# Three projections that carry the small stages behind them, and eight taps of a convolution on TensorE

## What is computed

```python
def nsa(h, w_in, ...):            # D = 1024, kv = 256, 16 heads
    q, kc, vc, ks, vs, kw, vw, gates = jnp.split(h @ w_in, splits, axis=-1)
    kc, vc = compress(kc, ...), compress(vc, ...)
    gates = jax.nn.sigmoid(gates)                       # 3 per head
    return (g0 * o_cmp + g1 * o_sel + g2 * o_win) @ w_out

def conformer_conv(val, gate, conv_w, ...):             # 31 taps, 512 channels
    u = val * jax.nn.sigmoid(gate)
    y = causal_depthwise_conv(u, conv_w) + conv_b
    return jax.nn.silu(layer_norm_2(y, ln_g, ln_b))

def fox_mix(h, w_in, fgate_b, q_g, k_g, w_out):
    q, k, v, fz = jnp.split(h @ w_in, [hd, 2 * hd, 3 * hd], axis=-1)
    q, k = rms_norm(heads(q), q_g), rms_norm(heads(k), k_g)
    c = jnp.cumsum(jax.nn.log_sigmoid(fz + fgate_b), axis=1)
    # causal softmax of q.k * scale + c[query] - c[key], times v, @ w_out

def third_mix(y, ...):
    q, k, v, gu, gv = jnp.split(y @ w_in, ...)          # 512 each
    attn_out = moba_attention(rope(q), rope(k), v)
    gv = layernorm(gelu(gv), gmlp_ln_g, gmlp_ln_b)
    gmlp_out = gelu(gu) * (causal(w_s) @ gv + b_s)      # per head, chunks of 128
    return concat([rmsnorm(attn_out, g_a), rmsnorm(gmlp_out, g_g)]) @ w_out
```

## Time and profile before

| | us |
|---|---|
| median of three runs | 4069.65 |
| lowest and highest | 4064.81, 4070.16 |
| the profiled execution | 4067.28 |
| its span | 4065.5 |
| PE busy | 3757.7 (92%) |
| DVE busy | 2986.4 (73%) |
| ACT busy | 1814.9 (45%) |
| mean TensorE clock granted | 0.953 |

### The profile page before, as it was taken

One profiled execution on the slowest core, in us unless ns is written; L12 is line 12 of the kernel. 1 busy time (PEld: TensorE's weight loads), 2 busy tenths in 40 slices (PEclk: granted clock), 3 DMA queues, 4 the chain that ended last, 5 costly groups with the idle time before them and its releaser, 6 DMA issues. The chain is left out here.

```text
span 4065.5 us, 72114 instructions
## 1 busy us (share of the span) xinstructions
PE 3757.7 (92%) x29143; PEld 3408.6 (84%) x29143; DVE 2986.4 (73%) x5894; ACT 1814.9 (45%) x3679; POOL 346.3 (9%) x259
## 2 busy tenths in 40 slices
PE   6999899997899769999999997998999999998698
PEld 6987799996799659989998885898999988897597
DVE  7876778785787677987677856589776787787665
ACT  3444445442454444434444454443444444544343
POOL 0000000000000004830000000086100000000000
PEclk9999899998799879999999997999999999999799
DMA  8766476764166414434444443343444444675253
GB/s 322 277 233 251 172 263 240 264 257 167 57 254 254 155 42 177 153 129 168 172 170 167 158 175 114 114 169 134 146 167 172 171 156 177 244 300 211 94 180 142
DMA packets 119358, 748.70 MB, mean 184 GB/s; under 512 B 13681, under 2 KB 13841, under 8 KB 43761
## 3 DMA queue, kind: packets, MB, share of 16 engines
q1 hardware_dynamic: 117506, 739.92, 49.6%
q10 hardware_dynamic: 688, 3.11, 0.2%
q0 software_dynamic: 832, 1.06, 0.1%
HBM read 741.93 MB, written 1.05 MB: 183 GB/s over the span
## 5 line engine op out<-in xcount | busy, mean ns | idle before, releaser
L930 ACT ACTIVATE weights_high<-weight_ring 128x512 fp32r<-128x512 f32 x2248 | 1294.6, 624 | 1225.6 <-PE bank L196 909.2
L938 DVE TENSOR_TENSOR weights_low<-weight_ring,weights_high 128x512 fp32r<-128x512 f32 x2016 | 1297.1, 686 | 613.4 <-ACT weights_high L930 607.8
L196 PE MATMUL bank<-h_high,weights_high 128*128 128x256 f32 x4800 | 1370.7, 286 | 31.7 <-DVE h_low L682 10.3
L196 PE MATMUL bank<-h_low,weights_high 128*128 128x256 f32 x4800 | 1362.7, 284 | 0.0
L196 PE MATMUL bank<-h_high,weights_low 128*128 128x256 f32 x4800 | 1362.3, 284 | 0.0
L196 PEld LDWEIGHTS bank<-h_high,weights_high 128*128 128x128 f32 x4800 | 924.8, 193 | 51.3 <-issue 27.4
L196 PEld LDWEIGHTS bank<-h_low,weights_high 128*128 128x128 f32 x4800 | 925.4, 193 | 8.7 <-issue 0.2
L196 PEld LDWEIGHTS bank<-h_high,weights_low 128*128 128x128 f32 x4800 | 924.9, 193 | 0.0
L196 PE MATMUL acc<-weights_high,hidden_high 128*128 128x512 f32 x1552 | 613.3, 395 | 0.0
L196 PE MATMUL acc<-weights_low,hidden_high 128*128 128x512 f32 x1552 | 606.4, 391 | 0.0
L196 PE MATMUL acc<-weights_high,hidden_low 128*128 128x512 f32 x1552 | 604.2, 389 | 0.0
(11 more groups left out here) (297 smaller groups left out, 3460.3 us busy)
## 6 DMA issues: line engine op xcount, KB each, us to landing
weight_ring<-stream SPq DMA_DIRECT2D x580, 1024.0 KB, 4.8
h_tok<-slots SPq DMA_DIRECT2D x100, 512.0 KB, 5.8
h_feat<-slots SPq DMA_DIRECT2D x90, 512.0 KB, 5.8
work<-slots SPq DMA_DIRECT2D x26, 512.0 KB, 8.4
mod_sums<-biases SPq DMA_DIRECT2D x7, 1536.0 KB
h_feat<-rows SPq DMA_DIRECT2D x8, 512.0 KB, 4.1
work<-biases SPq DMA_DIRECT2D x1, 1536.0 KB
x_tok<-x ACTq DMA_DIRECT2D x1, 1024.0 KB, 5.4
```

Source lines behind the costliest of these rows:

```text
L196: ins = self.nc.tensor.matmul(out, lhs, rhs, start=start, stop=stop)
L930: act.activation(k.w_hi[:, b, q * self.QUARTER:(q + 1) * self.QUARTER], self.raw(g, q), ACT.Copy).then_inc(k.highs_ready, 1)
L938: return eng.tensor_tensor(k.w_lo[:, b, w], self.raw(g, q), k.w_hi[:, b, w].bitcast(F32), ALU.subtract)
```

## The change

- NSA: the narrow stage goes. `ToFeatureRowsAndGates` makes the 16 f32 products of the gates in four parts, behind the products of halves 8 to 11, into another bank, and ScalarE takes the sigmoid from there behind half 11. Their weights are no longer in the slot stream: `DirectRows` loads them in front of slot s + 3. The features stage sums twelve modulation slots from half 6 on, the tokens stage none. The four row copies of GpSimd move to the `Scores` of the first branch, the compressed branch comes last.
- Even mix: the last eight taps of channel block 2 leave VectorE. ScalarE makes eight more diagonals at the end of `GlaDecays`, TensorE does eight f32 products of 128x256 between key and value products of `GlaAttend`, VectorE adds the result at its end.
- Fox: `ToTokens`, `ToTokensNarrow`, `HeadNorm` and `ForgetGates` become `ToNormedHeads`. VectorE multiplies by the gains as it evicts, ScalarE squares, VectorE reduces block by block; root, scaling, gates, cumulative sums and the filling of constant rows are set to single halves.
- Third mix: `ToTokens`, both `Keep`, `Rope`, `Spatial` and the second `HeadRms` become `ToTokensAndGate`, whose columns come in the order gv, gu, q, k, v. The causal mask of the mixing weights comes at half 3, layer norm at halves 4 to 8, spatial products behind half 10, gates at 10 and 12, norm at 13 to 16, rotation of the two token tiles at 17 and 18. It sums four slots; `third_ffn(0)` sums 14 in halves 50 to 66.

The stream has 575 slots instead of 581, and 49 stages end in a barrier instead of 58. The core of the diff:

```diff
+class DirectRows:
+    def issue(self, sp, biases, slots, rows):
+        self.host.wait_begun(sp)
+        for i, place in enumerate(self.places):
+            n = place.shape[1]
+            sp.dma_start(place, rows[self.first + i][:, 0:n]).then_inc(self.k.direct_landed, 16)
...
+class ToFeatureRowsAndGates(ToFeatureRows):
+    FIRST = 8
+    def products(self, pe, g, hi, lo):
+        k, part = self.k, g - self.FIRST
+        super().products(pe, g, hi, lo)
+        if part == 0:
+            self.direct.wait(pe)
+        if 0 <= part < 4:
+            t, half, w = part // 2, part % 2, self.gates.shape[2]
+            for kk in range(half * DC // 2, (half + 1) * DC // 2):
+                mm = k.mm(k.acc[:, t, 0:w], k.h_t[:, kk, t * P:(t + 1) * P], self.kept[:, kk * w:(kk + 1) * w],
+                          start=kk == 0, stop=kk == DC - 1, last=True)
...
+class ToNormedHeads(ToTokens):
+    def vector_after(self, dve, g):
...
+        elif g % 4 == 3:
+            for t in range(TT):
+                a = slice(b * 512, (b + 1) * 512)
+                dve.wait_ge(k.scalar_for_vector.sem, k.scalar_for_vector.take())
+                dve.tensor_tensor(self.qk[:, t, a], k.bank[:, (TT * b + t) % NB, :], self.gains[:, a],
+                                  ALU.mult).then_inc(k.vector_for_tensor.sem, k.vector_for_tensor.send())
+        if g % 4 == 0 and 0 < b <= self.N:
...
+            ins = dve.tensor_reduce(stat, squares, AX, ALU.add)
...
+        self.gates.vector(dve, g)
+        piece = g - 4 * self.N - 2
+        if 0 <= piece < 4:
...
+            dve.tensor_tensor(heads, heads, self.stat[:, at:at + n // 2].unsqueeze(2).to_broadcast([P, n // 2, HD]),
+                              ALU.mult)
...
 class Convolve:
+    LATE = 8
...
+    def late_products(self, pe):
+        k, c = self.k, CONV // P - 2
+        for i in range(self.LATE):
+            tap = TAPS - self.LATE + i
+            pe.wait_ge(k.diagonals, TAPS + i + 1)
+            mm = k.mm(k.acc[:, 3, 0:S], self.late[i], self.u[:, c, tap:tap + S], start=i == 0,
+                      stop=i == self.LATE - 1, last=True)
...
+class ToTokensAndGate(ToTokens):
+    def vector_after(self, dve, g):
+        k = self.k
+        super().vector_after(dve, g)
+        if g == 3:
+            self.keep(dve)
+        if 4 <= g <= 8:
+            self.norm(dve, g - 4)
+        if g == 10:
...
+            self.gate(dve, 0)
+        if g == 12:
+            self.gate(dve, 1)
+        if 13 <= g <= 16:
+            self.root_mean_square(dve, g - 13)
+        if g == 17:
+            self.rope(dve, 0)
+        if g == 18:
+            dve.wait_ge(k.scalar_for_tensor.sem, self.taken[self.K, 1])
+            self.rope(dve, 1)
...
-    features = ToFeatureRows(k, feat, 20, scaled=DC, scale=HD ** -0.5)
+    features = ToFeatureRowsAndGates(k, feat, 20, DC, HD ** -0.5, gates,
+                                     p.rearrange("p a b -> p (a b)")[:, 0:DC * 3 * H])
...
-    features.carry(k.sums[5], 10, turning, 8, 20)
-    projected = ToTokensAndCouples(k, [(v, None)], feat[:, DC:DC + 4, :], couples)
-    projected.carry(k.sums[5], 2, turning, 0, 4)
-    narrow = ToTokensNarrow(k, [(3 * H, gates, ACT.Sigmoid)])
...
+    features.carry(k.sums[5], 12, turning, 6, 20)
+    projected = ToTokens(k, [(v, None)])
...
-        layers.carry(k.sums[8], 8, (0, 1, 2, 3), 50, 66)
+        layers.carry(k.sums[8], 14, (0, 1, 2, 3), 50, 66)
...
-    projected.carry(k.sums[8], 10, (0, 1, 2, 3), 0, 20)
-    keep = [Keep(k, extra), Keep(k, norms)]
+    projected = ToTokensAndGate(k, gv, gu, qk, v, extra, norms, k.h_tok[:, :, 512:], own, tmp)
+    projected.carry(k.sums[8], 4, (2, 3), 0, 4)
```

504 lines of the change are left out of this document (340 added, 164 removed).

## The result

The changed kernel takes 4024.20 us (median of three, 4017.48 to 4025.36) against 4069.65; the ratio is 0.9887, 95% interval 0.9865 to 0.991. The prediction was 4003 with a range of 3993 to 4019: 45 us are gained, 21 fewer than forecast. The profiled execution took 4025.36 us, its span is 4023.3 us (4065.5 before), so it is 42.2 us shorter where 66.5 were forecast.

| part | before | after | change | forecast |
|---|---|---|---|---|
| stretch that ends with the NSA features | 517.5 | 524.8 | +7.3 | +5.7 |
| NSA tokens stage | 21.4 | 11.9 | -9.5 | -9.5 |
| NSA narrow stage | 5.2 | | -5.2 | -5.1 |
| compression and the three attention branches | 136.4 | 150.7 | +14.3 | -0.5 |
| decays, scaling, attention of GLA | 50.9 | 51.6 | +0.7 | -0.5 |

A forecast was written before the change was run, and what follows sets the result against it. TensorE, busy 92% of 4065.5 us, was taken as the bound, its idle stretches as the gain. NSA -9.4, even mix -0.5, Fox -28.7, third mix -28.9 and feed-forward +1.0 gave -66.5: 4003 us, range 3993 to 4019.

The forecast's parts named there:

- The bound: Whole kernel: TensorE works 92% of the 4065.5 us span; a change can take only the stretches where it stands still.
- the removed stages: Stages taken out: NSA narrow stage -5.1 us, Fox -33.4, third mix -32.8; the NSA tokens stage shortens by 9.5.
- The clock: Rival: stretches next to emptied stages regain clock, 6 to 9 us more than the counted 2.2, about 3995; chance 0.13.
- behind the diagonals: Even mix: the stage after the lengthened decay stage may start at half clock, +0.4 us.
- cover fails: Rival: inserted steps wait, low parts come late and TensorE stalls, 10 to 20 us, 4013 to 4023; chance 0.22.
- The first feed-forward with 14 slots: Feed-forward ahead of the third mix: six more slots bring VectorE nearly to the bound, +1.0 us, bounds 0 and 5.
- The third projection: Third mix: 54.4 us plus 3.6 for spatial products and 1.5 for the tail, 59.5 us.
- the tail: End of the third projection: key rotation makes it end 2.2 us after the products instead of 0.7, +1.5 us.
- The first slot of the NSA features: NSA features: slot wait of 3.7 us makes low part 7 1.6 us late; with 0.5 at half 8, +2.1 us.
- the gates: NSA features: 32 narrow products move between the halves at full clock with nothing hiding them, +3.6 us.
- The taps: Even mix: eight fewer taps shorten GLA attention by 2.6 us, extra diagonals lengthen the decay stage by 1.7; net -0.5.
- Fox: Fox part: -33.4 us of stages, +5.2 of products in the projection, -0.5 of clock behind it; sum -28.7 us.

The follow-up runs named there:

- e2: Changed kernel plus four unread f32 products of 128x64 behind the transposes of the two NSA branches; 4013.73 us.
- e6: Repeat, for its times, of the changed kernel with four unread products behind the transposes of the two NSA branches; 4012.12 us.
- e3: Changed kernel with the third projection's direct rows issued in front of slot s + 4 instead of s + 3; 4011.35 us.
- e11: Changed kernel with fillers, later direct rows, early diagonals, NSA slots from half 8, reordered third-projection tail and early square-root table load; 3995.82 us.
- e4: Changed kernel with the eight late diagonals made by ScalarE ahead of its wait for the gate logits; 4014.18 us.
- e1: Changed kernel once more, unaltered, with its own profile; 4025.7 us median.

## Why the prediction was wrong

**The bound and the removed stages** were right: every stage said to go went with its length (71.4 us, and 9.5 of the tokens stage), and the features, tokens, decay and attention stages came out within 1.6 us of the forecast.

The clock was in the prediction as a rival with the sign of a gain, and as a loss only behind the diagonals (0.4 us): I read the rows at 0.50 as something to be won back and did not ask of the rows at 1.00 whether they were safe. None of my rows was of a `Values` stage. With the two stages at full clock the kernel takes 4010.7 to 4015.5 us (e2 and e6), within the range, but still some 10 us above the 4003; the rest is in the terms below.

**A second term stood at nothing**: what a wait of TensorE costs beyond its length. Behind a wait of 2.3 us in the NSA features, and again behind a second one of 3.1 us in the third projection, the clock was at half for 3.4 us, 1.4 and 1.6 us of work lost. My sums took such waits at their bare length. The trace of the kernel before had the case, behind the wait of 4.0 us for low parts at the start of its third projection:

```profile
3699.70:3703.10 3.40, 3.40 (x10) 2.66 (x9) 2.91 (x5) 0.90 (x2) 0.00 (x0) 0.50 1.02 420
```

The rival "cover fails" has the measured 4024 inside its 4009 to 4025, but that is luck. Two late low parts did come, 5.4 us of waits and some 3 of clock, but the larger part of the miss, 14.7 us, is in the Values stages, of which it says nothing.

The Trainium skill ("TensorE: Matmul & The Clock Gate", The HAM clock gate) ties the clock to sustained activity. The trace agrees in the rise, 3.9 us after the first transpose, and shows besides that 0.7 us of idle time can be followed, 2.7 us later, by a fall in full work, and that 15.7 us of full work can then go by at half clock.

**The first feed-forward with 14 slots** was put at +1.0 with bounds 0 and 5. It cost nothing: from its start to the first product of the projection 1036.0 us before and after. In the six halves of the earlier trace rows VectorE has 16.86 of 17.00 us now, as counted (16.9), and TensorE is full; it waits for no low part in this feed-forward's last halves, so no slot came late:

```profile
3613.03:3630.03 17.00, 17.00 (x122) 16.02 (x121) 16.86 (x29) 7.51 (x14) 0.00 (x0) 1.00 1.01 402
```

**The third projection** was mis-sized by 5.7 us. 3.2 are more wait of TensorE (7.3 us for 4.0), since the direct rows stand in SP's queue between the second and the third slot; as a term of the sum they were at nothing, though "cover fails" names them. 1.6 are a second 3.4 us at half clock behind that wait, which e3 removes with it. Another 0.5 us is the tail (2.7 us behind the last product for 2.2); 0.4 are left over. The norm that stays pays 1.3 us for a table load that the removed spatial stage had paid; e11 takes it away.

**The first slot of the NSA features** landed as forecast: VectorE waited 3.4 us for it, for 3.7. But the addition that it has to follow ended at 893.5 and not at 891.8, since VectorE waited 1.6 us for the residual's rows (0.5 before), and TensorE waited 2.3 us for low part 7 instead of 1.6; at half 8 it did not wait. The rest of the +7.3 is 3.6 for the gates, as forecast, and the 1.4 of clock behind the wait. In e4, where the clock stayed up, the stretch is 5.7 us longer than before, which is the forecast, but by other terms.

**The taps**: -2.6 and +1.7 were both right; the clock in the next stage cost 1.7 us, which I had at 0.4.

**Fox** came out better. The stretch grew by 3.5 us instead of 5.2, and what follows, from ToHeads on, gained 2.6 instead of 0.5, both by clock:

```profile
2420.00:2493.70 73.70, 71.13 (x331) 58.60 (x330) 48.67 (x76) 45.16 (x74) 0.00 (x0) 1.00 0.54 194
```

The projection is full from its first product on at clock 1.00 (0.98 before: 3.4 us at half clock behind a wait of 1.9 us, which the changed kernel has too, without the fall). VectorE is at 48.7 and ScalarE at 45.2 us, close to the 46.6 and 41 of the count: the cover held in all 24 halves. The stage of ToHeads itself takes 9.7 us as before; the gain is in the transposes and the output projection behind it.

## What to carry to other kernels

When a change moves stages, ask of each stage behind them not only what it does but at which clock it ran and what lies just ahead of it; a barrier of 0.7 us ahead of a stage of light products cost ten times its length here, and four unread products behind the last useful one removed that. Price a wait of TensorE at its length and the half clock behind it. What is loaded directly has a place in a queue: put it behind whatever is needed first. Repeat the changed kernel unaltered before explaining a difference by the change.

## What the runs showed of the hardware

The same `Values` stage, 96 products, took 12.7 us in some profiles and 20.0 to 20.3 us in others, by the clock alone. Single executions of the unaltered changed kernel on one chip spread over 20 us (4013.7 to 4033.9, e1); two such stages account for 14.7 of it. In the sixteen stages of the two branches without fillers the slow case came with a rise of the clock 3.5 to 4.1 us after the first transpose (ten of ten) and never with a later one; in Fox, with the same idle time of 0.72 us, rises at 3.1 to 3.2 us (seven) and at 5.1 to 6.1 us (seven) were all followed by full clock. Longer waits of TensorE, 2.3, 3.1 and 4.0 us, were followed by 3.4 us at half clock in full work; one of 1.55 us (e4, NSA) was not, and one of 1.9 us ahead of the Fox projection was in the kernel before and not in the changed one.
